# A state-space and expert layer on one core: B matrices on the sync queue, coarse powers and the state maps of rounds 1 to 5 on VectorE

## The reference

```
step  = exp(log_step);  a_bar = exp(lam * step)
b_bar = ((a_bar - 1) / lam) * (b_re + i b_im)
bu    = einsum('blgk,gpk->blgp', u, b_bar)
s     = associative_scan over time of  s_t = a_bar * s_{t-1} + bu_t      (forward, and backward)
y     = real(einsum('blgp,gkp->blgk', s_f + s_b, c)) + u * d
```

## Time and profile before

| What | Value |
|---|---|
| Median of three runs | 2064.38 us (2064.05 to 2069.93) |
| Profiled execution | 2067.78 us, span 2066.0 us |
| TensorE busy | 1885.0 us, 91% |
| VectorE, ScalarE, GpSimd busy | 674.5, 394.1, 273.1 us |
| Chain that ended last | PE 49%, DMA 39%, DVE 4%, ACT 2% |

### The profile page before, as it was taken

How to read it: one execution, slowest core, us unless ns; L and a number is a source line. 1 busy time by engine, 2 the same in 40 slices (tenths; PEclk the granted TensorE clock), 3 DMA queues, 4 the chain that set the end, 5 groups by cost and what they waited for, 6 DMA issues and landing times.

```text
span 2066.0 us, 20072 instructions
## 1 busy us (share of the span) xinstructions
PE 1885.0 (91%) x8396; PEld 922.8 (45%) x8396; DVE 674.5 (33%) x1178; ACT 394.1 (19%) x708; POOL 273.1 (13%) x279
## 2 busy tenths in 40 slices
PE   8999999999999997998888979988898988978997
PEld 3556578566688753333333323333333333333332
DVE  5799769798856342001001000100100100100103
ACT  1434312399710131000000000000000000000001
POOL 2887430265300000000000000000000000000001
PEclk9999999999999998999999999999999999999999
DMA  6422313234242677999999999999999999999995
GB/s 158 130 84 68 116 55 113 88 122 127 94 173 92 238 297 288 403 429 432 431 432 432 432 432 432 432 430 432 432 432 431 431 431 431 432 431 432 432 423 231
DMA packets 79594, 638.16 MB, mean 309 GB/s; under 512 B 20572, under 2 KB 34320, under 8 KB 61456
## 3 DMA queue, kind: packets, MB, share of 16 engines
q1 hardware_dynamic: 66864, 628.99, 73.8%
q10 hardware_dynamic: 12640, 7.89, 1.4%
HBM read 626.98 MB, written 9.88 MB: 308 GB/s over the span
## 4 chain that ended last, share of the span: by engine, by line
PE 49%; DMA 39%; DVE 4%; ACT 2%; issue 1%; POOL 0%; DVEq 0%; SPq 0%; ACTq 0%
PE ps L1159 48%; DMA arena<-in_w_e 39%; DVE arena L2052 1%; ACT arena L790 1%; ACT L790 0%; PE ps L1276 0%; PE ps L1670 0%; DVE arena L2374 0%; DMA gate_scratch<-arena 0%; DVE arena L2049 0%; POOL arena L613 0%; DVE arena L2339 0%; PE ps L1422 0%; DVE arena L2368 0%; DVE arena L2274 0%
## 5 line engine op out<-in xcount | busy, mean ns | idle before, releaser
L1159 PE MATMUL ps<-arena 128*64 128x512 f32 (+7 forms) x7794 | 1810.7, 522 | 145.3 <-DMA arena<-in_w_e 125.7
L1159 PEld LDWEIGHTS ps<-arena 128*64 128x64 f32 (+2 forms) x7794 | 852.3, 159 | 1071.6 <-issue 869.1
L790 ACT ACTIVATE arena<-ps 128x512 f32<-128x512 f32 (+5 forms) x306 | 170.1, 581 | 1534.3 <-PE ps L1159 901.7
L2339 DVE TENSOR_TENSOR arena<-arena,ps 128x512 f32<-128x512 f32 (+1 forms) x48 | 30.3, 644 | 692.0 <-PE ps L1159 692.0
L782 POOL TENSOR_TENSOR arena<-arena 128x1024 f32<-128x1024 f32 x3 | 7.1, 2353 | 1351.0 <-ACT arena L790 1351.0
L2348 DVE TENSOR_TENSOR arena<-arena,ps 128x512 f32<-128x512 f32 x48 | 33.1, 690 | 402.5 <-PE ps L1159 402.5
L790 ACT ACTIVATE arena<-arena 128x128 f32<-128x128 f32 (+11 forms) x261 | 118.5, 509 | 83.1 <-DVE arena L2052 29.1
L790 ACT ACT_TABLE_LOAD x73 | 93.7, 1283 | 32.5 <-issue 27.4
L2052 DVE SCALAR_TENSOR_TENSOR arena<-arena 128x512 f32<-128x512 f32 x80 | 62.4, 780 | 2.8
L723 POOL TENSOR_TENSOR arena<-arena 128x768 f32<-128x768 f32 x16 | 28.4, 1778 | 142.0 <-PE ps L1367 91.1
L1670 PE MATMUL ps<-arena 128*128 128x128 f32 x176 | 25.7, 295 | 7.0 <-DVE arena L2339 5.9
(11 more groups left out here) (229 smaller groups left out, 767.3 us busy)
## 6 DMA issues: line engine op xcount, KB each, us to landing
arena<-in_w_e SPq DMA_DIRECT2D x76, 5632.0 KB, 28.8
arena<-in_w_e SPq DMA_DIRECT2D x15, 2816.0 KB, 26.0
arena<-in_w_e SPq DMA_DIRECT2D x26, 1408.0 KB, 15.3
arena<-in_w_in SPq DMA_DIRECT2D x9, 2048.0 KB, 8.5
arena<-in_w_e SPq DMA_DIRECT2D x12, 1536.0 KB, 17.3
arena<-cumulative_scratch SPq DMA_DIRECT2D x16, 768.0 KB, 4.9
arena<-in_w_in SPq DMA_DIRECT2D x5, 1536.0 KB, 7.0
arena<-in_w_out_ssd SPq DMA_DIRECT2D x4, 1536.0 KB, 6.7
```

The lines of the kernel that those rows point to most:

```text
L790: return act.activation(out, in_, func, **kw)
L1159: return pe.matmul(out, lhsT, rhs, start=a, stop=z)
L2339: tt(o, o, ps[:, 3 + i, 0:w], ALU.mult).then_inc(s.hid_ready, 1)
```

## The change

It moves three things and computes the same.

- The two B matrices (48 groups x 64 states x 16 values each, runs of 64 bytes) are loaded from SP, behind the first two w_in slices and ahead of the third, instead of from ScalarE behind its other parameters.
- The coarse powers are formed by VectorE, behind its state maps 0 and ahead of output maps 1, as two fills and three doublings (`coarse_powers`); GpSimd forms the fine powers and then waits for them (`rot_ready` 2).
- The state maps of rounds 1 to 5 are formed by VectorE: those of round 1 behind the step decays and ahead of the first recursion, those of rounds 2 to 5 directly behind the output maps of the same round. GpSimd forms none.

```
@@ SP
-            slices(0, FIRST_GATE)
+            slices(0, NW)
+            for r, name in enumerate(("s5_b_re", "s5_b_im")):
+                sp.dma_start(b_raw[:, r], A[name][0].rearrange("(g b) p k -> (b p) g k", b=2)).then_inc(s.b_loaded, 16)
+            slices(NW, FIRST_GATE)
@@ GpSimd
             powers(fine, 0)
-            powers(coarse, FINE.bit_length() - 1)
-            maps_tmp = pool_tmp...
+            pool.wait_ge(s.rot_ready, 2)
             for q in range(NQ):
                 for d in range(2):
                     ...
-                for q_ in ([1] if q == 0 else []) + ([q + 2] if q + 2 < NQ else []):
-                    state_maps(pool, n, [maps_tmp[:, i, :] for i in range(4)], q_)
@@ ScalarE
-            for r, name in enumerate(("s5_b_re", "s5_b_im")):
-                act.dma_start(b_raw[:, r], ...).then_inc(s.b_loaded, 16)
@@ VectorE, behind its state maps 0
+            def coarse_powers():
+                n.done(dve.memset(coarse[:, 0, :, 0:1], 1.0))
+                n.link(dve.memset(coarse[:, 1, :, 0:1], 0.0))
+                m = 1
+                while m < NC // FINE:
...
+                    tt(t[0], x[0], turn[0], ALU.mult)
+                    tt(t[1], x[1], turn[1], ALU.mult)
+                    tt(t[2], x[0], turn[1], ALU.mult)
+                    n.link(tt(t[3], x[1], turn[0], ALU.mult))
+                    n.done(tt(o[0], t[0], t[1], ALU.subtract))
+                    r = tt(o[1], t[2], t[3], ALU.add)
+                    m *= 2
...
+            coarse_powers()
@@ VectorE, the rounds
                     maps(q + 1)
                 if q == 0:
                     time_steps()
+                if 1 <= q < NQ - 1:
+                    state_maps(dve, n, [...], q + 1)
...
                 toeplitz_rows(q)
                 if q == 0:
                     step_decays()
+                    state_maps(dve, n, [...], 1)
```

More of the change, by code:

```diff
@@ L694, in _ @@
             powers(fine, 0)
-            powers(coarse, FINE.bit_length() - 1)
-            maps_tmp = pool_tmp.rearrange("p a b -> p (a b)").rearrange("p (i c) -> p i c", i=4)
+            pool.wait_ge(s.rot_ready, 2)
             for q in range(NQ):
@@ L813, in _ @@
             act.dma_start(d_row, A["ssd_d"][0].partition_broadcast(P)).then_inc(s.broadcasts_loaded, 16)
-            for r, name in enumerate(("s5_b_re", "s5_b_im")):
-                act.dma_start(b_raw[:, r], A[name][0].rearrange("(g b) p k -> (b p) g k", b=2)).then_inc(s.b_loaded, 16)
             act.wait_ge(s.par_ready, 1)
@@ L1899, in _ @@
             state_maps(dve, n, [x.rearrange("p g c -> p (g c)")[:, 0:QB * 64] for x in (zr, zi, t1, t2)], 0)
+            def coarse_powers():
[3 more added lines that the diff above has]
+                while m < NC // FINE:
+                    k = FINE.bit_length() - 1 + m.bit_length() - 1
+                    turn = [last(rot[:, r, k].rearrange("p d g -> p (d g)"), m) for r in range(2)]
+                    t = [x.rearrange("p g c -> p (g c)")[:, 0:2 * GP * m].rearrange("p (g j) -> p g j", j=m) for x in (zr, zi, t1, t2)]
+                    x, o = ([coarse[:, r, :, m0:m0 + m] for r in range(2)] for m0 in (0, m))
+                    tt(t[0], x[0], turn[0], ALU.mult)
[5 more added lines that the diff above has]
+                    m *= 2
+                    if m < NC // FINE:
+                        n.link(r)
+                    else:
+                        r.then_inc(s.rot_ready, 1)
+                        n.wait()
+                dve.wait_ge(s.rot_ready, 2)
+            coarse_powers()
             def time_steps():
@@ L1962, in _ @@
                     time_steps()
+                if 1 <= q < NQ - 1:
+                    state_maps(dve, n, [x.rearrange("p g c -> p (g c)")[:, 0:QB * 64] for x in (zr, zi, t1, t2)], q + 1)
                 if q == 1:
@@ L1969, in _ @@
                     step_decays()
+                    state_maps(dve, n, [x.rearrange("p g c -> p (g c)")[:, 0:QB * 64] for x in (zr, zi, t1, t2)], 1)
                 for d in range(2):
```

## The result

The changed kernel takes 2078.61 us (2076.66 to 2079.69) beside 2064.22 for the kernel before: ratio 1.0069, 95% interval 1.0056 to 1.0083, or 14.4 us slower where 12.8 was forecast. In the profiled executions it is 2079.13 us against 2067.78, 11.35 more.

What follows compares the result with a forecast made beforehand. TensorE sets the pace, 33.84 us a round, VectorE having 3.5 to spare. Recursions end at 116.9, plus 38.3 and three rounds of 37.8: 268.6, 12.8 later than 255.8; 2064.4 + 12.8 = 2077, range 2061 to 2086.

Steps and rivals of the forecast that it cites:

- VectorE's first chain earlier: At the start, with ScalarE freed of the B transfer, VectorE's L1826 comes 5.3 or 4.3 us earlier; 5.0 taken.
- TensorE gains at the start: Near 28 to 38 us, TensorE regains a 3.8 us gap and 3.05 us of lower clock: 6.85 us, bounds 0 to 6.85.
- Coarse powers take, end: VectorE's 18 short operations alternate with GpSimd's fine powers from 59.55: 12.3 us, done at 71.9; about 4.5 us by themselves.
- TensorE waits near 80: TensorE's second gate tile waits for VectorE's time steps: idle 5.3 us from 78.6, plus 3.05 us for the lower clock.
- State maps beside the table: Rounds 2 to 5: VectorE's twelve operations beside GpSimd's second table take 10.0 us; bounds 4.5 and 15.
- rival 1: ScalarE's input blocks hold TensorE's second gate tile too, 3 us every second round plus lower clock: +19, 2083; chance 0.12.
- rival 2: Collision costs the front only; state maps stay near 4.5 us, rounds are TensorE's again: -1.6, 2063, no change; chance 0.17.
- rival 4: The change doesn't free ScalarE: B matrices on SP's queue delay the parameters, start unchanged: +18, 2082; chance 0.08.
- The strict rule: VectorE operations with two SBUF inputs and GpSimd's SBUF reads exclude each other: state maps 11.3, round 39.1, five us more.
- the one-for-one price: Beside a GpSimd table, VectorE's operations alternate with GpSimd's at 1.26 us each: 6.4 of them in 8.05 us.
- The prediction's sign of being right: TensorE waits for VectorE's L1954 before each set of transposes, with VectorE's rounds at 37 to 38 us.
- rival 3: No alternation for VectorE's short and medium operations; TensorE keeps its gains in front, rounds 33.84: -10, 2054; chance 0.13.

## Why the prediction was right

Step by step, forecast and measured (us from the start of the span):

| Step | Forecast | Measured |
|---|---|---|
| VectorE's first chain earlier | 5.0 | 4.1 |
| TensorE gains at the start | 6.85 | 5.9, at its state products of round 0 (66.63 for 72.53) |
| Coarse powers take, end | 12.3, 71.9 | 11.1, 71.4 |
| Output maps 1 end, time steps | 82.4, 83.9 | 82.23, 83.69 |
| TensorE waits near 80 | 5.3, and a lower clock | 4.13, and a lower clock behind it |
| First recursions | 95.3 to 116.9 | 94.21 to 115.78 |
| State maps beside the table | 10.0 | 9.95 |
| Round 1, later rounds | 38.3, 37.8 | 38.08, 37.6 |
| End of the last recursion | 268.6 | 266.7 |
| TensorE's round-5 state products later | 12.8 | 12.2 |

The range, 2061 to 2086, also holds the times of rivals 1, 2 and 4, so the time alone tells little; the steps and the experiments carry the account.

The mechanism holds: by the ratios, holding the table alone took back 10.9 us of 14.2, and putting the state maps back on GpSimd took back all of it within the interval. Time steps and Gelu, moved out of the way, took back nothing.

The size of the state maps' term came from one price, VectorE's and GpSimd's operations ending about one for one, read where output maps ran beside a table. The strict rule, by which VectorE loses the whole table, gave 11.3 for it and a round of 39.1; the measured 9.95 and 37.6 are those of the one-for-one price. Alone, the twelve operations and the table take 4.5 and 6.8 us, 11.3 together; ended in 9.95, they did in part run at the same time. The copy of the earlier trace rows that the prediction set beside that rule has one SBUF input where the rule speaks of two; the rows that bear on it are those of the earlier trace rows. The SBUF page (the Trainium skill, SBUF — State Buffer, who interferes with whom) is borne out in two other points: operations with two SBUF inputs contend with GpSimd's reads, and those with at most one, outside the modes in which VectorE uses both ports, don't (0.69 us in the recursion beside a table, with the other operand in PSUM). One SBUF input is not enough to be safe, though: the Toeplitz copies have one, and take 1.14 us beside a table and 0.24 alone.

Rival 1 was set apart too sharply from the forecast. ScalarE did hold TensorE, by 0.24, 2.87, 1.83 and 2.87 us, and after two of these two gate tiles took 15.70 instead of 14.00. But most of that fell into time in which TensorE would have waited for the recursion. What is left is the last round, where TensorE starts its state products at 267.95, 1.3 after VectorE is done; VectorE itself was 1.9 earlier than forecast, so two small errors nearly cancel. The prediction's sign of being right, that TensorE waits for the recursion before each set of transposes, came true in rounds 2 and 4 and not in rounds 3 and 5, where ScalarE had made TensorE later than VectorE. There the sum was right in size partly by luck: its last step has the recursion release TensorE's state products, and it was ScalarE's delay that set them.

Rivals 2 and 3 fell with the measured 9.95, rival 4 with ScalarE's activation at 24.36. Something of rival 4 is true: the parameters came 1.2 us later (20.21 for 18.97). That is why VectorE's first chain gained 4.1 us although ScalarE's table load ran ahead of its wait, a case for which the prediction had 5.3; TensorE, whose first u tile begins behind the same copies (22.41 for 21.17), gained 5.9 and not 6.85. What was not forecast is that the gain at the start is worth so little: the B matrices alone shorten the front by some 3 us and the median by nothing that can be measured. Nor is the stretch behind the rounds as constant as the sum takes it: 12.2 us at the state products came out as 14.4 in the medians.

## What to carry to other kernels

Before moving work to the engine with spare time, ask what the engine it leaves will run beside it: here 4.5 us of work became 9.95 because it landed on a table of GpSimd, and that was more than VectorE's 3.5 us of slack. Put GpSimd's long operations beside VectorE work that has an operand in PSUM; a copy from SBUF to SBUF pays as well. Removing a wait in front of a stage that another engine paces only moves the wait, as the time steps and the Gelu showed.

## What the runs showed of the hardware

- After an equal wait of 1.61 us TensorE's next 58 matmuls took 13.42 us in one execution and 16.40 in another of the same kernel, with a granted clock of 0.83 around the longer ones (1.00 in the shorter case). Of all thirteen traces of this case eight have 13.42, three 14.77 to 14.92 and two 16.39 and 16.40. A price read once for a fall of the clock is a price that is paid sometimes.
- The two engines pay unequally for the overlap: a table took 7.7 us beside the state maps (121.31 to 129.03) and 7.2 beside short operations (82.40 to 89.55), where it takes 6.8 alone, while VectorE's state maps went from 4.5 to 9.95.
- A ScalarE table load ran ahead of the wait of the activation that needs it (load at 19.34, activation at 24.36 after 3.74 us of waiting), so it was free.
